# A chain of transformer-like stages on one core: order of the work at the norm boundaries, and which engine adds LayerNorm's mean

## The chip, the cores and the metric

One core of one Trainium2 chip. The metric is the time in microseconds (us) from start to end of one execution. The kernel holds a whole model of 21 stages in one program; its weights come from HBM piece by piece, while the activations (1024 features of 512 tokens) stay in SBUF.

## What is computed

Two stacks of two layers in fp32: the first with RMS norms in front of its mixers and FFNs, the second with LayerNorm behind each sum.

```python
def rms_norm(x, g):
    xf = x.astype(F32)
    y = xf * lax.rsqrt(jnp.mean(xf * xf, axis=-1, keepdims=True) + NORM_EPS)
    return (y * g.astype(F32)).astype(x.dtype)

def layer_norm(x, g, b):
    xf = x.astype(jnp.float32)
    mu = jnp.mean(xf, axis=-1, keepdims=True)
    var = jnp.mean(jnp.square(xf - mu), axis=-1, keepdims=True)
    return ((xf - mu) * lax.rsqrt(var + LN_EPS) * g + b).astype(x.dtype)

def swiglu_2(x, w_in, w_out):
    gu = x @ w_in
    g, u = gu[..., :D_FF], gu[..., D_FF:]
    return (jax.nn.silu(g) * u) @ w_out
...
    for l in range(DEPTH):
        x = layer_norm(ALPHA * x + 0.5 * swiglu_2(x, ffn_w_in[l, 0], ffn_w_out[l, 0]), ln_g[l, 0], ln_b[l, 0])
        j = l // N_MIXERS
        if l % N_MIXERS == 0:
            y = mlstm_mixer(x, ml_w_in[j], ml_gate_b[j], ml_norm_g[j], ml_w_out[j])
        else:
            y = window_attention(x, at_w_in[j], at_sink[j], at_w_out[j])
        x = layer_norm(ALPHA * x + y, ln_g[l, 1], ln_b[l, 1])
        x = layer_norm(ALPHA * x + 0.5 * swiglu_2(x, ffn_w_in[l, 1], ffn_w_out[l, 1]), ln_g[l, 2], ln_b[l, 2])
```

## The kernel before

Layout. Features lie on the 128 partitions, in KD = 8 tiles of 128; the T = 512 tokens lie on the free axis and are taken at a norm in two halves of 256 (HALVES). R holds the residual. Each fp32 operand is split into a high and a low part (XH and XL, HH and HL, WH and WL), and each product is three matmuls: lines 310, 311 and 312 (pe_three).

Weights come in units of 128 x 1024. SyncE loads unit n into a ring of RING = 6 places RAW once unit n - 6 is done (unit_done), ScalarE copies it to WH (hi_to, line 292), VectorE subtracts and writes WL over RAW (lo_to, line 298). Both keep count: hi_to(n) and lo_to(n) split what is missing up to unit n.

Stages: load, ev_attn, ev_mamba, n_ffn0, ffn0, n_mix1, od, n_ffn1, ffn1, n_final, f00, ln00, mlstm, ln01, f01, ln02, f10, ln10, win, ln11, f11. Nine are norms between other stages: n_ffn0, n_mix1, n_ffn1 and n_final are RMS norms, five are LayerNorms. Behind ("prod") ln00, ln02, ln10, n_mix1 and n_final stands an FFN, behind the others a mixer.

End of an FFN (ffn_pe, lines 465 to 482). down(m) multiplies the hidden features (22 k-tiles) into output tile m in three units, k-tiles 0 to 8, 8 to 16 and 16 to 22. The last tile (m = 7) is done once for each token half; between the first and the second unit of its second half TensorE does stats_pe (line 402): column sums of S1 and R (LayerNorm alone) and of S2 and the last SQ, against a matrix of ones, into PSUM banks 4 and 5. S1 and S2 are sums over the tiles that VectorE keeps in finish (line 688), SQ the squares that ScalarE makes (square_act, line 484). A mixer's output projection (outproj_pe) does its last three tiles by halves; stats_pe of half 0 stands behind the first of the second half.

The norm itself, per half h: VectorE waits for the sums, makes the variance (chain, line 830), ScalarE the reciprocal root (root, line 618), VectorE a Newton step and NB = -mean times root. Then for each tile t (0 to 7 in half 0, 8 to 15 in half 1), in a buffer XT of four places:
- VectorE: XT = R * RS (normed, line 854)
- LayerNorm alone, GpSimd: XT = XT + NB (line 549)
- ScalarE: R = g * XT + b where the residual is kept (line 633), XH = g * XT + b (line 635)
- VectorE: XL = R - XH (low, line 860; 862 in an RMS norm without keep)
- TensorE waits for x_ready of the tile

VectorE's order is written out in norm (line 847): three tiles of normed ahead, then normed(t + 3), low(t); behind t = 2 the last tile or tiles of the second half of the stage before (ffn_tail(1) or mixer_tail(1)); lo_to(nx + 4) behind t = 5; chain(e, 1) behind t = 7; lo_to(nx + 5) behind t = 10 and lo_to(nx + 6) behind t = 13. nx is the first unit of the next stage. ScalarE does hi_to at the same t, and the squares of the second half behind t = 3.

The next stage begins with first_units (line 334): three units together over half 0 (per k-tile 9 matmuls of 256 columns), stats_pe of half 1 behind k = 4, the fourth unit over half 0, then all four units over half 1 (12 matmuls per k-tile). Before each k-tile TensorE waits for its XL.

## Time and profile before

| what | us |
|---|---|
| median of 3 runs | 3537.15 (3535.1 to 3537.25) |
| time of the profiled execution | 3536.34 |
| its span, first to last instruction | 3534.5 |
| TensorE busy | 3431.3 (97%) |
| VectorE busy | 1842.6 (52%) |
| ScalarE busy | 1308.0 (37%) |
| GpSimd busy | 92.8 (3%) |
| mean granted TensorE clock | 0.991 |

Times in the rows further down are us from the start of the span. PE is TensorE, DVE is VectorE, ACT is ScalarE, POOL is GpSimd. A row of a timeline is start, duration, engine, line, operation, what it writes and reads, shape, count and, in brackets, the idle time before it and what ended it. Matmuls overlap, so that their pace is read from their starts.

### The profile page before, as it was taken

How to read it: one execution, taken by the hardware profiler on the slowest of the kernel's cores; microseconds unless marked ns; L12 is line 12 of the kernel's file. 1: busy time of each engine (PE TensorE's matmuls, PEld its weight loads, DVE VectorE, ACT ScalarE, POOL GpSimd, SP SyncE). 2: the span in 40 equal slices, each digit the busy share in tenths (PEclk: the TensorE clock that was granted, in tenths of full speed). 3: DMA queues.
4: the chain of work that ended last, by engine and by line, in shares of the span. 5: the costliest groups of instructions: out<-in, count | busy, mean ns of one | idle time of the engine just before them, and what ended most of it. 6: DMA issues, size and time to landing. Idle time of an engine off the chain costs nothing.

```text
span 3534.5 us, 43300 instructions
## 1 busy us (share of the span) xinstructions
PE 3431.3 (97%) x17564; PEld 2827.1 (80%) x17564; DVE 1842.6 (52%) x2925; ACT 1308.0 (37%) x2217; POOL 92.8 (3%) x133
## 2 busy tenths in 40 slices
PE   8999999999998999999999999999999999999998
PEld 7667778888876988898888768888888888788887
DVE  5775775433885644354435357443454336564446
ACT  4442443222465322242224344322242226543233
POOL 0000000000100000000001001000010001010000
PEclk9999999999999999999999999999999999999999
DMA  3102112323210222322332201232322331013245
GB/s 127 59 24 95 60 60 90 100 96 107 88 37 20 95 96 96 107 96 96 97 105 81 99 31 54 102 101 96 107 85 96 101 106 64 31 49 125 95 138 166
DMA packets 92506, 307.59 MB, mean 87 GB/s; under 512 B 16014, under 2 KB 17684, under 8 KB 92308
## 3 DMA queue, kind: packets, MB, share of 16 engines
q1 hardware_dynamic: 89528, 301.31, 25.4%
q10 hardware_dynamic: 2780, 3.51, 0.3%
q8 instruction: 140, 2.29, 0.3%
q14 instruction: 58, 0.48, 0.0%
HBM read 302.69 MB, written 2.10 MB: 86 GB/s over the span
## 4 chain that ended last, share of the span: by engine, by line
PE 82%; DVE 11%; ACT 4%; issue 2%; DMA 0%; SPq 0%; DVEq 0%; POOL 0%; ACTq 0%
PE ps L310 23%; PE ps L311 23%; PE ps L312 23%; PE ps L307 13%; DVE XT L854 1%; DVE WL L298 1%; ACT WH L292 1%; DVE mb_cv L1786 1%; PE ps L2768 1%; DVE XL L860 1%; DVE R L699 1%; DMA RAW<-units 0%; DVE S L708 0%; DVE mb_e L1847 0%; PE ps L1097 0%
## 5 line engine op out<-in xcount | busy, mean ns | idle before, releaser
L310 PE MATMUL ps<-XH,WH 128*128 128x512 f32 (+1 forms) x3200 | 1189.7, 372 | 34.2 <-DVE XL L860 23.6
L312 PE MATMUL ps<-XH,WL 128*128 128x512 f32 (+1 forms) x3200 | 1173.9, 367 | 0.0
L311 PE MATMUL ps<-XL,WH 128*128 128x512 f32 (+1 forms) x3200 | 1173.8, 367 | 0.0
L298 DVE TENSOR_TENSOR WL<-RAW,WH 128x1024 fp32r<-128x1024 f32 x567 | 688.3, 1228 | 313.8 <-ACT WH L292 310.1
L310 PEld LDWEIGHTS ps<-XH,WH 128*128 128x128 f32 x3200 | 609.0, 190 | 142.6 <-DVE XL L860 16.8
L312 PEld LDWEIGHTS ps<-XH,WL 128*128 128x128 f32 x3200 | 609.0, 190 | 97.3
L311 PEld LDWEIGHTS ps<-XL,WH 128*128 128x128 f32 x3200 | 609.5, 190 | 95.8 <-issue 1.9
L292 ACT ACTIVATE WH<-RAW 128x1024 fp32r<-128x1024 f32 x567 | 587.3, 1050 | 146.0 <-DMA RAW<-units 80.2
L310 PE MATMUL ps<-HH,WH 128*128 128x512 f32 (+1 forms) x990 | 362.8, 366 | 0.0
L311 PE MATMUL ps<-HL,WH 128*128 128x512 f32 (+1 forms) x990 | 361.9, 366 | 0.0
L312 PE MATMUL ps<-HH,WL 128*128 128x512 f32 (+1 forms) x990 | 361.9, 366 | 0.0
L589 ACT ACTIVATE HH<-HV 128x512 fp32r<-128x512 f32 x132 | 83.4, 632 | 566.2 <-DVE HV L773 566.2
L770 DVE SCALAR_TENSOR_TENSOR SG<-TH,ps 128x512 f32<-128x512 f32 x132 | 90.7, 687 | 299.4 <-ACT TH L586 299.2
L773 DVE SCALAR_TENSOR_TENSOR HV<-SG,ps 128x512 f32<-128x512 f32 x132 | 90.7, 687 | 297.0 <-PE ps L312 296.8
L699 DVE SCALAR_TENSOR_TENSOR R<-R,ps 128x512 f32<-128x512 f32 (+1 forms) x86 | 51.6, 599 | 361.2 <-PE ps L312 360.6
L490 ACT ACTIVATE SQ<-R 128x512 f32<-128x512 f32 (+1 forms) x89 | 49.0, 551 | 509.9 <-DVE R L699 432.1
L586 ACT ACTIVATE TH<-ps 128x512 f32<-128x512 f32 x132 | 78.7, 596 | 368.5 <-PE ps L312 368.5
L310 PEld LDWEIGHTS ps<-HH,WH 128*128 128x128 f32 x990 | 186.7, 189 | 30.3
L311 PEld LDWEIGHTS ps<-HL,WH 128*128 128x128 f32 x990 | 186.7, 189 | 30.3
L312 PEld LDWEIGHTS ps<-HH,WL 128*128 128x128 f32 x990 | 186.7, 189 | 30.0
L775 DVE TENSOR_TENSOR HL<-HV,HH 128x512 fp32r<-128x512 f32 x132 | 91.4, 693 | 101.4 <-ACT HH L589 101.4
L549 POOL TENSOR_TENSOR XT<-XT,NB 128x256 f32<-128x256 f32 x80 | 74.8, 949 | 2082.1 <-DVE XT L854 2082.1
(607 smaller groups left out, 3438.5 us busy)
## 6 DMA issues: line engine op xcount, KB each, us to landing
RAW<-units SPq DMA_DIRECT2D x567, 512.0 KB, 3.3
XIN<-in_x ACTq DMA_DIRECT2D x2, 1024.0 KB, 6.1
out<-YT SPq DMA_DIRECT2D x8, 256.0 KB, 3.1
GB<-in_ln_g SPq DMA_DIRECT2D x1, 512.0 KB
GB<-in_ln_b SPq DMA_DIRECT2D x1, 512.0 KB
da_pi<-in_positions ACTq DMA_DIRECT2D x1, 256.0 KB, 3.1
mb_pairf<-constants ACTq DMA_DIRECT2D x1, 256.0 KB
wa_dist<-constants ACTq DMA_DIRECT2D x1, 192.0 KB, 2.2
```

The lines of the kernel that those rows point to most:

```text
L292: nc.scalar.activation(WH[:, u % RING, :], RAW[:, u % RING, :], ACT.Copy).then_inc(S["wh_ready"], 1)
L298: nc.vector.tensor_tensor(WL[:, u % RING, :], RAW[:, u % RING, :], WH[:, u % RING, :].bitcast(F32), ALU.subtract)\
L307: return nc.tensor.matmul(out, lhsT, rhs, start=start, stop=stop, **kw)
L310: nc.tensor.matmul(out, wh, xh, start=start, stop=False)
L311: nc.tensor.matmul(out, wh, xl, start=False, stop=False)
L312: return nc.tensor.matmul(out, wl, xh, start=False, stop=stop)
L586: nc.scalar.activation(TH[:, j % 2, :], ps[:, 2 * (j % 3), :], ACT.Tanh, scale=0.5).then_inc(S["ffn_act"], 1)
L589: nc.scalar.activation(HH[:, j, :], HV[:, j % 2, :], ACT.Copy).then_inc(S["ffn_act"], 1)
L699: own(v.scalar_tensor_tensor(rk, rk, alpha, src, ALU.mult, ALU.add), "r_ready")
L770: own(v.scalar_tensor_tensor(SG[:, j % 2, :], TH[:, j % 2, :], 1.0, ps[:, b, :], ALU.add, ALU.mult))
L773: own(v.scalar_tensor_tensor(HV[:, j % 2, :], SG[:, j % 2, :], e["half"], ps[:, b + 1, :], ALU.mult, ALU.mult), "ffn_dve")
L775: own(v.tensor_tensor(HL[:, j, :], HV[:, j % 2, :], HH[:, j, :].bitcast(F32), ALU.subtract), "ffn_dve")
```

## The change

Four parts, all at the norm boundaries.
- down_parts: the last output tile of an FFN takes its short unit (k-tiles 16 to 22) first, in the list of units too. stats_pe of half 0 still stands behind the first unit.
- Sums and variance: stats_pe signals behind S1 and R and again behind S2 and SQ (stats_ready counts 4 per LayerNorm), and VectorE's first two operations wait for the first signal alone. square_added, the adding of tile 6's squares into S2, stands ahead of the wait for the last tile. stats_pe of half 1 stands behind k = 3 (FFN behind) or k = 5 (mixer behind) in a LayerNorm.
- NB is added by VectorE, and GpSimd's loop is gone. VectorE takes tiles in pairs (one operation over two tiles) but for the first two of each half; low is paired too in part.
- The order on VectorE and ScalarE is written out anew: hi_to(nx + 4) directly behind root(0), lo_to(nx + 4) after tile 4, 5 (LayerNorm) or after the variance of half 1 (RMS), lo_to(nx + 5) behind low(9).

```diff
@@ def down_parts
+def down_parts(m):
+    return ((16, 22), (0, 8), (8, 16)) if m == KD - 1 else ((0, 8), (8, 16), (16, 22))
@@ first_units
+            stats_at = 4 if not nrm.get("ln") else 3 if nrm["prod"]["kind"] == "ffn" else 5
...
-                elif k == 4:
+                elif k == stats_at:
                     stats_pe(pe, nrm, 1)
@@ stats_pe
-                mm(ps[:, 4, hs], ones[:], R[:, KD - 1, hs], False, True)
+                mm(ps[:, 4, hs], ones[:], R[:, KD - 1, hs], False, True).then_inc(S["stats_ready"], 1)
@@ ffn_pe
-                for q, (k0, k1) in enumerate(parts):
+                for q, (k0, k1) in enumerate(down_parts(m)):
@@ gpsimd
-                if e["kind"] == "norm" and e["ln"]:
-                    for t in range(16):
-                        x = XT[:, t % 4, :]
-                        pool.wait_ge(S["ln_scaled"], 16 * lns + t + 1)
-                        nc.gpsimd.tensor_tensor(x, x, NB[:, t // 8, :], ALU.add).then_inc(S["t_ready"], 1)
-                    lns += 1
@@ scalar, norm
                 root(0)
+                hi_to(act, nx + 4)
+                squares_at = 3 if not e["ln"] else 4 if prod["kind"] == "ffn" else 5
...
-                    if t == 3:
+                    if t == squares_at:
                         for q in range(KD, KD + prod["tail"]):
                             square_act(act, prod, q)
-                    if t in (5, 10, 13):
-                        hi_to(act, nx + {5: 4, 10: 5, 13: 6}[t])
+                    if t in (10, 13):
+                        hi_to(act, nx + {10: 5, 13: 6}[t])
@@ vector
                     else:
+                        square_added(e, KD - 2)
                         dve.wait_ge(S["tail_done"], e["t0"] + 1)
...
-            def chain(e, h):
+            def variance(e, h):
...
                 if e["ln"]:
+                    dve.wait_ge(S["stats_ready"], e["st0"] + 2 * h + 1)
                     own(v.tensor_scalar(a, s1, 1.0 / D, None, ALU.mult))
                     own(v.tensor_tensor(a, a, s1, ALU.mult))
+                    dve.wait_ge(S["stats_ready"], e["st0"] + 2 * h + 2)
                     own(v.scalar_tensor_tensor(x, s2, D * LN_EPS, a, ALU.add, ALU.subtract), "var_ready")
...
+                def normed(t, n=1):
                     k, h = t % 8, t // 8
+                    x = XT[:, t % 4:t % 4 + n, :]
+                    wide = lambda a: a[:, h:h + 1, :].to_broadcast([P, n, HT])
+                    own(v.scalar_tensor_tensor(x, R[:, k:k + n, HALVES[h]], D ** 0.5, wide(RS), ALU.mult, ALU.mult),
+                        None if ln else "t_ready")
+                    if ln:
+                        own(v.tensor_tensor(x, x, wide(NB), ALU.add), "t_ready", by=n)
...
+                variance(e, 0)
+                rooted(e, 0)
+                if ln:
+                    normed(0)
+                    normed(1)
+                    low(0)
+                    normed(2, 2)
+                    low(1)
+                    normed(4, 2)
+                    low(2)
+                    low(3)
+                    if ffn_behind:
+                        ffn_tail(1)(e["prod"])
+                        normed(6, 2)
+                        low(4, 2)
+                    else:
+                        mixer_tail(1, (0,))(e["prod"])
+                        low(4, 2)
+                        mixer_tail(1, (1, 2))(e["prod"])
+                        normed(6, 2)
+                    lo_to(dve, nx + 4)
+                    variance(e, 1)
+                    low(6, 2)
+                    rooted(e, 1)
+                    normed(8)
+                    normed(9)
+                    low(8)
+                    normed(10, 2)
+                    low(9)
+                    lo_to(dve, nx + 5)
+                    normed(12, 2)
+                    low(10, 2)
+                    normed(14, 2)
+                    low(12, 2)
+                    lo_to(dve, nx + 6)
+                    low(14, 2)
+                else:
+                    normed(0)
+                    for t in range(8):
+                        if t < 7:
+                            normed(t + 1)
+                        low(t)
+                        if t == 2:
+                            (ffn_tail if ffn_behind else mixer_tail)(1)(e["prod"])
+                    variance(e, 1)
+                    lo_to(dve, nx + 4)
+                    rooted(e, 1)
...
```

rooted(e, h) is the rest of chain: it waits for the root, does the Newton step and NB.

## Rows read from the trace of the kernel before

**Rows 1.** The page, busy time, share of the span, instructions of TensorE.
```profile
PE 3431.3 (97%) x17564; PEld 2827.1 (80%) x17564; DVE 1842.6 (52%) x2925; ACT 1308.0 (37%) x2217; POOL 92.8 (3%) x133
```

**Rows 2.** Waits of TensorE: for whom; us in total, times, longest.
```profile
PE ps L310 <- DVE XL L860: 23.6, 17, 2.4
...
PE ps L310 <- DVE XL L862: 3.0, 2, 2.7
```

**Rows 3.** Timeline of TensorE at ln00 (last rows ln01, ln02): start, us, instruction, idle before.
```profile
1902.41 0.28 PE L312 MATMUL ps<-HH,WL 128*128 128x256 f32 x1
1902.54 0.59 PE L307 MATMUL ps<-S,ones 128*128 128x256 f32 x2
...
1911.84 0.35 PE L310 MATMUL ps<-XH,WH 128*128 128x256 f32 x1 [2.39 <-DVE XL L860]
...
1928.08 0.39 PE L310 MATMUL ps<-XH,WH 128*128 128x256 f32 x1 [1.31 <-DVE XL L860]
...
1933.23 0.39 PE L310 MATMUL ps<-XH,WH 128*128 128x256 f32 x1 [0.57 <-DVE XL L860]
...
2212.74 0.39 PE L310 MATMUL ps<-XH,WH 128*128 128x256 f32 x1 [0.57 <-DVE XL L860]
...
2562.47 0.36 PE L310 MATMUL ps<-XH,WH 128*128 128x256 f32 x1 [2.38 <-DVE XL L860]
```

**Rows 4.** Timeline of VectorE at ln00, then ln01 and ln02.
```profile
1892.66 0.69 DVE L703 TENSOR_TENSOR S<-S,R 128x512 f32<-128x512 f32 x1
...
1901.78 1.22 DVE L298 TENSOR_TENSOR WL<-RAW,WH 128x1024 fp32r<-128x1024 f32 x1 [0.78 <-ACT WH L292]
1904.46 0.42 DVE L836 TENSOR_SCALAR VA<-ps 128x256 f32<-128x256 f32 x1 [1.45 <-PE ps L307]
...
1908.19 2.62 DVE L854 SCALAR_TENSOR_TENSOR XT<-R,RS 128x256 f32<-128x256 f32 x4
1911.26 0.42 DVE L860 TENSOR_TENSOR XL<-R,XH 128x256 fp32r<-128x256 f32 x1 [0.45 <-DVE XT L854]
...
1930.27 0.42 DVE L860 TENSOR_TENSOR XL<-R,XH 128x256 fp32r<-128x256 f32 x1
1930.73 1.64 DVE L298 TENSOR_TENSOR WL<-RAW,WH 128x1024 fp32r<-128x1024 f32 x1
...
1932.75 0.43 DVE L860 TENSOR_TENSOR XL<-R,XH 128x256 fp32r<-128x256 f32 x1
...
2177.86 2.36 DVE L298 TENSOR_TENSOR WL<-RAW,WH 128x1024 fp32r<-128x1024 f32 x2
...
2555.11 0.42 DVE L836 TENSOR_SCALAR VA<-ps 128x256 f32<-128x256 f32 x1 [1.46 <-PE ps L307]
...
2583.30 0.42 DVE L860 TENSOR_TENSOR XL<-R,XH 128x256 fp32r<-128x256 f32 x1
```

**Rows 5.** Timeline of ScalarE at ln00: root, XH, weight copy.
```profile
1905.83 0.42 ACT L621 ACTIVATE RS<-VA 128x256 f32<-128x256 f32 x1 [2.64 <-DVE VA L838]
...
1910.21 0.58 ACT L635 ACTIVATE XH<-XT,VEC 128x256 fp32r<-128x256 f32 x1
...
1929.00 1.05 ACT L292 ACTIVATE WH<-RAW 128x1024 fp32r<-128x1024 f32 x1
```

**Rows 6.** Timeline of GpSimd at ln00.
```profile
1908.77 3.51 POOL L549 TENSOR_TENSOR XT<-XT,NB 128x256 f32<-128x256 f32 x4 [888.58 <-DVE XT L854]
```

**Rows 7.** Windows: busy us of five engines, PEclk, DMA share, GB/s.
```profile
1890.00:1940.00 50.00, 45.74 (x345) 44.42 (x344) 37.10 (x61) 26.86 (x47) 14.91 (x16) 0.97 0.16 50
2170.00:2222.00 52.00, 46.62 (x331) 44.28 (x330) 42.95 (x73) 29.80 (x53) 14.96 (x16) 0.93 0.13 42
2548.00:2592.00 44.00, 39.29 (x299) 37.38 (x298) 33.16 (x56) 24.92 (x44) 14.96 (x16) 1.00 0.13 41
...
1120.80:1124.10 3.30, 3.30 (x9) 2.58 (x8) 0.00 (x0) 0.00 (x0) 0.00 (x0) 0.50 0.00 0
```

**Rows 8.** Timeline of TensorE in the stage od.
```profile
1119.27 0.50 PE L310 MATMUL ps<-od_gh,WH 128*128 128x512 f32 x1 [3.56 <-ACT od_y L2380]
```

**Rows 9.** The page, DMA issues: KB each, us from issue to landing.
```profile
RAW<-units SPq DMA_DIRECT2D x567, 512.0 KB, 3.3
```

More of the change, by code:

```diff
@@ L37, in knows, with __call__ @@
         self.n.update(dict.fromkeys(sems, 0))
-    def __call__(self, ins, name=None, wait=True):
+    def __call__(self, ins, name=None, wait=True, by=1):
         name = name or self.steps
-        ins.then_inc(self.sems[name], 1)
-        self.n[name] = self.n[name] + 1
+        ins.then_inc(self.sems[name], by)
+        self.n[name] = self.n[name] + by
         if wait:
@@ L72, in unit_lists @@
             for m in range(0 if s.get("last") else KD):
-                units += [tile(d, di, P * m, 0, 8), tile(d, di, P * m, 8, 16), tile(d, di, P * m, 16, 22)]
+                units += [tile(d, di, P * m, k0, k1) for k0, k1 in down_parts(m)]
         elif kind == "ev_attn":
@@ L703, in finish, with square_added @@
                     own(v.tensor_tensor(S1[:, hs], R[:, 0, hs] if m == 1 else S1[:, hs], rk, ALU.add))
-                if q and 0 < e["tiles"][q - 1][0] < KD - 1:
-                    m, h = e["tiles"][q - 1]
+                if not squares_in:
+                    square_added(e, q - 1)
+            def square_added(e, q):
+                if q >= 0 and 0 < e["tiles"][q][0] < KD - 1:
+                    m, h = e["tiles"][q]
                     hs = slice(0, T) if h is None else HALVES[h]
-                    dve.wait_ge(S["sq_ready"], e["sq0"] + q)
+                    dve.wait_ge(S["sq_ready"], e["sq0"] + q + 1)
                     own(v.tensor_tensor(S2[:, hs], SQ[:, 0, hs] if m == 1 else S2[:, hs], SQ[:, m % 2, hs], ALU.add), "s2_added")
@@ L714, in go, with mixer_tail @@
                     else:
+                        square_added(e, KD - 2)
                         dve.wait_ge(S["tail_done"], e["t0"] + 1)
-                    finish(e, KD - 1 + h, ps[:, 7 - h, HALVES[h]], e["alpha"])
+                    finish(e, KD - 1 + h, ps[:, 7 - h, HALVES[h]], e["alpha"], squares_in=True)
                 return go
-            def mixer_tail(h):
+            def mixer_tail(h, some=range(3)):
                 def go(e):
-                    for i in range(3):
+                    for i in some:
                         m = KD - 3 + i
@@ L843, in chain, with low @@
                 if e["ln"]:
-                    own(v.scalar_tensor_tensor(NB[:, h, :], s1, -(D ** -0.5), y, ALU.mult, ALU.mult))
+                    own(v.scalar_tensor_tensor(NB[:, h, :], ps[:, 4, HALVES[h]], -(D ** -0.5), y, ALU.mult, ALU.mult))
             def norm(e):
-                ln, final, nx = e["ln"], e["final"], e["next"]
-                def normed(t):
+                ln, nx = e["ln"], e["next"]
+                ffn_behind = e["prod"]["kind"] == "ffn"
+                def normed(t, n=1):
                     k, h = t % 8, t // 8
-                    if final and t >= 4:
-                        dve.wait_ge(S["norm_r"], e["nr0"] + t - 3)
-                    x = XT[:, t % 4, :]
-                    own(v.scalar_tensor_tensor(x, R[:, k, HALVES[h]], D ** 0.5, RS[:, h, :], ALU.mult, ALU.mult), "ln_scaled" if ln else "t_ready")
-                def low(t):
+                    x = XT[:, t % 4:t % 4 + n, :]
[4 more added lines that the diff above has]
+                        own(v.tensor_tensor(x, x, wide(NB), ALU.add), "t_ready", by=n)
+                def low(t, n=1):
                     k, hs = t % 8, HALVES[t // 8]
-                    dve.wait_ge(S["xh_ready"], 16 * e["c"] + t + 1)
+                    dve.wait_ge(S["xh_ready"], 16 * e["c"] + t + n)
                     if ln or e["keep"]:
-                        own(v.tensor_tensor(XL[:, k, hs], R[:, k, hs], XH[:, k, hs].bitcast(F32), ALU.subtract), "x_ready")
+                        own(v.tensor_tensor(XL[:, k:k + n, hs], R[:, k:k + n, hs], XH[:, k:k + n, hs].bitcast(F32), ALU.subtract),
+                            "x_ready", by=n)
                     else:
@@ L863, in low @@
                                                    XH[:, k, hs].bitcast(F32), ALU.mult, ALU.subtract), "x_ready")
-                ahead = 3 if ln and not final else 1
-                chain(e, 0)
-                for t in range(ahead):
-                    normed(t)
-                for t in range(16):
-                    if t + ahead < (8 if t < 8 else 16):
-                        normed(t + ahead)
-                    if not final:
-                        low(t)
-                    if t == 2:
-                        second.get(e["prod"]["kind"], mixer_tail(1))(e["prod"])
-                    if t == 5:
-                        lo_to(dve, nx + 4)
-                    if t == 7:
-                        chain(e, 1)
-                        for i in range(8, 8 + ahead):
-                            normed(i)
-                    if t in (10, 13):
-                        lo_to(dve, nx + {10: 5, 13: 6}[t])
+                variance(e, 0)
@@ new lines, in norm @@
+                rooted(e, 0)
[38 more added lines that the diff above has]
+                            normed(t + 1)
+                        low(t)
+                        if t == 2:
[3 more added lines that the diff above has]
+                    rooted(e, 1)
+                    normed(8)
+                    for t in range(8, 16):
+                        if t < 15:
+                            normed(t + 1)
+                        low(t)
+                        if t in (10, 13):
+                            lo_to(dve, nx + {10: 5, 13: 6}[t])
```

16 lines of the change are left out of this document (9 added, 7 removed).

## The prediction

> **What bounds the kernel now.** I read the page first, for the engine that fills the span: TensorE is busy 3431.3 of 3534.5 us [rows 1]. So only the some 100 us in which it waits can be won. The waits of TensorE come next: its longest entry is one helper line, L860, the low part XL of the normalised tiles, 23.6 us in 17 waits [rows 2]. L860 runs in the LayerNorms and in n_final; the RMS line L862 is worth 3.0 us in 2 waits. So the change works on some 24 us at five LayerNorm boundaries. Three have an FFN behind them (ln00, ln02, ln10), two a mixer (ln01, ln11).
>
> Then the time order of ln00. TensorE issues the column sums at 1902.54, works through its cover (14 k-tiles, 42 matmuls 0.12 us apart) and waits 2.39 us until XL of tile 0 is there; then 1.31 us before token half 1 and 0.57 us at its tile 3 [rows 3]. VectorE in the same time is a chain without room: variance, root, Newton, four scalings that take 2.62 us together, XL [rows 4]. ScalarE is the station between [rows 5]. GpSimd's first four adds last 3.51 us [rows 6]. A scaling takes 0.42 us alone and up to 0.84 us beside a GpSimd add (four take 2.62, not 4 x 0.46 = 1.84).
>
> What ends the boundary is the last of these waits. XL of tile 11 (half 1, k = 3) ends at 1932.75 + 0.43 = 1933.18, TensorE goes on at 1933.23 and has five tiles of 12 matmuls (1.43 us each) left: 1940.4. In a mixer boundary it is the same wait, at 2212.74 [rows 3].
>
> The clock: the windows of the boundaries read 0.97 for ln00, 0.93 for ln01 and 1.00 for ln02, the level lies at 0.50 in the stretch after a wait of 3.56 us elsewhere [rows 7, 8], and each low stretch costs some 1.7 us of matmul work (0.07 x 52 = 3.6 us for ln01's two). Yet this does not set the end today: from the variance to XL of tile 11 ln00 takes 1932.75 - 1904.46 = 28.29 us with a low stretch, ln02 2583.30 - 2555.11 = 28.19 us without one [rows 4]. VectorE sets the end, and a slow TensorE uses up its own waiting.
>
> **The change part by part, for ln00** (times of the trace; an operation of VectorE 256 wide counts 0.46 with its handing over, one 512 wide 0.72, from L703's 0.69 [rows 4]; XT to XH over ScalarE 0.03 + 0.50 + 0.58, and 0.10 back to VectorE [rows 5]).
>
> Short unit first: 18 matmuls stand ahead of the sums instead of 24, so they start 0.72 us sooner, at 1901.8. The cover grows by the same six matmuls and ends where it did, at 1909.3.
>
> Sums and variance sooner: the first two operations no longer wait for the squares, which would bring 0.9 us, but VectorE has a weight split until 1903.0 [rows 4]. So they run from 1903.0, the third from 1904.0. The variance is ready at 1904.4 instead of 1905.8: 1.4 us.
>
> Mean by VectorE: NB is ready at 1906.75. Scaling and add of tile 0 (2 x 0.46) end at 1907.6; GpSimd's ended near 1909.7, when ScalarE took over. XH is ready at 1908.7 and XL of tile 0 at 1909.25 (1911.68 before). TensorE's first wait of 2.39 us is gone.
>
> What is late next: now each pair of tiles costs VectorE 2 x 0.72 before the next XL. XL of tiles 1 and 2 come 1.91 us apart (1.45 + 0.46), and TensorE needs 1.08 us for a tile (9 matmuls): 0.83 us of waiting, twice. The squares and sums of half 1 move ahead (ScalarE squares after tile 4, TensorE sums after k = 3, near 1915.3), and VectorE takes the half's last tile before its pair 6, 7: hidden, since TensorE is busy with k = 1 to 3. XL of tiles 6 and 7 stands behind the variance of half 1: 0.4 us. Half 0 ends at about 1924.5, 2.2 us sooner than before, and half 1 starts without its 1.31 us.
>
> Half 1, k = 2: here I see a new wait. The order on VectorE is: normed(10, 2), low(9), lo_to(nx + 5), normed(12, 2), low(10, 2). The split in lo_to waits for its WH, which ScalarE makes after XH of tile 10. Behind that waiting split stand two wide operations and XL of 10 and 11, for which TensorE waits. In numbers: normed(10, 2) ends at 1925.3, XH of 10 at 1926.4, WH (1.04 us, [rows 5]) at 1927.4; the split (1.14) at 1928.6, the pair (1.45) at 1930.0, XL of 10 and 11 at 1930.74. TensorE wants tile 10 two tiles after 1924.5, at 1927.4: 3.4 us of waiting. Before, XL of tile 10 came at 1930.27 + 0.42 = 1930.69, ahead of the split: the same time. From 1930.8 six tiles are left, 8.6 us: 1939.4 against 1940.4. So 1.0 us is won at each FFN boundary, while the clock stays up.
>
> Mixer boundaries: the short unit does not exist there, and in ln01 VectorE has two splits until 2180.2, until after the sums are done [rows 4], so the variance is no sooner. The same steps from there give a first wait of 1.06 us, 0.83 twice, some 3 us before tiles 6 and 7 (they stand behind a variance whose sums TensorE issues only after its tile 5), XL of 10 and 11 at 2211.0 and the end at 2219.7 against 2212.74 + 5 x 1.43 = 2219.9: 0.2 us won.
>
> The clock after the new wait: a wait of 3.4 us is longer than all of these boundaries had. After the comparable one of 3.56 us the clock was 0.50 [rows 7, 8]. A low stretch costs about 1.7 us of work; now it lies behind the last wait, where nothing takes it up. I take 1.6 us for each of the five, bounds 0 (ln02 had a wait of 2.38 us [rows 3] and kept 1.00) and 3.3 (two stretches).
>
> ScalarE's early weight split (hi_to right behind root 0) waits for a DMA: issue to landing is 3.3 us [rows 9], issued when the short unit is done near 1902.0, so it lands near 1905.3 and the copy ends near 1906.3, before the first XT at 1907.6: cost 0, covered by the Newton steps. Should the DMA be 1.3 us later it would delay XH directly. SP's order and all DMA sizes stay. RMS boundaries: their order hardly moves, they wait 3.0 us together, the larger part behind a mixer's tail that stays where it is: 0, bounds -0.5 and +0.5 for all four.
>
> The pairs' price is not in the trace (512 elements in two rows of 256, one operand repeated). Bounds: two single operations, 0.84 + 0.07 us (nothing saved), and L703's 0.69. I take 0.69, the nearest row in size. The chain up to XL of tile 10 has 13 wide operations (five pairs scaled and shifted, three pairs of XL); at the upper bound each lasts 0.19 us more, up to 2.5 us per boundary, +12 us in all.
>
> The sum: 3 x 1.0 + 2 x 0.2 = 3.4 us won, 5 x 1.6 = 8.0 us lost to the clock: +4.6 us on the profiled execution's 3536.34, 3540.9. The median of the runs shown lies 0.8 us higher, so I say 3541.5 us, 0.12% slower than 3537.15. A measurement of this kernel can tell about 0.2%, 7 us, from no change.
>
> **The rivals.**
> (A) The new wait does not arise: XL of 10 and 11 gets there in time, because ScalarE is far enough ahead with WH. Then TensorE runs through from 1924.5: 8 x 1.43 gives 1936.0, 4.4 us won per FFN boundary and 3.6 per mixer boundary, 20.4 us: 3536.3 + 0.8 - 20.4 = 3517. For it: half 0 does run 2 us sooner, and VectorE loses all contention. Against: WH stands behind XH of tile 10 in ScalarE's order, and that needs normed(10, 2).
> (B) The clock costs nothing, as in ln02. Then 3.4 us stay won: 3533.5. Speaking for it is that 2.38 us of waiting there left the level at 1.00; against it the stretch behind 3.56 us. The Trainium skill (TensorE: Matmul & The Clock Gate, "What's actually happening") calls the low level the state of an idle array, which activity releases; read strictly, a wait between working stretches would cost no clock. By that rule it is this rival; ln00 and ln01, 0.97 and 0.93 with waits of at most 2.4 us, speak against the strict reading.
> (C) Slower: the clock falls twice per boundary. The two waits of 0.83 us in 2.8 us, and in the mixers a wait of 3 us, lie early in half 0. A low stretch there delays the sums of half 1 by up to 1.7 us; VectorE has about 1 us of room before its variance, and from there on the whole chain moves. It decides once more than that 1 us is lost. Price: 0.7 to 1.7 us more at each boundary, 3.5 to 8.5 in all: 3545 to 3550. The pairs at their upper bound would end in the same place.
> (D) The change does nothing that can be seen: the gain and the clock cancel, within 2 us of 3537. This lies within my own case.
>
> **How the numbers follow.** My case with (D): 0.45 (3535 to 3544.2); B: 0.12; A: 0.16; C: 0.27. B falls wholly within 0.2%, and A nearly wholly outside it. C begins at its very edge: 0.03 of it stay below 3544.2, and I give my own case 0.03 above (a second low stretch at some boundaries). Faster by over 0.2% (below 3530.1): A's 0.16 and 0.01 of B, 0.17. Slower (above 3544.2): 0.24 + 0.03 = 0.27. Within: the rest, 0.56. The range leaves out A and the far end of C: 3530 to 3549.
>
> **What would show it.** Right, if in the profile after: GpSimd is idle at the boundaries and scalings take 0.42 us; sums of ln00 start 0.7 us sooner; the first wait of an FFN boundary is near 0 and two of 0.8 us follow; VectorE idles 1.7 us before the split in half 1 and TensorE 3 us or more at tile 10; the clock of ln02's window falls from 1.00. Wrong, if TensorE shows no wait over 1 us in half 1 (then A), or if paired operations last over 0.8 us (then C), or if the windows keep 1.00 behind the long wait (then B). A sum that misses by more than 10 us with these waits all in place would mean that something outside the norms moved.

## The result and the profile after

| | before | after |
|---|---|---|
| median, us | 3536.24 (3533.1 to 3539.75, 22 runs) | 3542.55 (3539.57 to 3545.52, 22 runs) |
| profiled execution: time, span, us | 3536.34, 3534.5 | 3542.36, 3540.2 |
| GpSimd busy, us | 92.8 | 18.4 |
| TensorE's waits for XL of the normalised tiles (LN), us, times | 23.6, 17 | 31.1, 22 |

The changed kernel takes 1.0019 of the time of before, 95% interval 1.0013 to 1.0025: 6.3 us, or 0.18%, slower. The interval does not hold 1, but the difference is small for a kernel of this length. The forecast was 3541.5 us in a range of 3530 to 3549. GpSimd's adds are gone and so is the first long wait, and yet the time is longer. First the page, engine times, and the waits of TensorE (for whom; us in total, times, longest):

```profile
span 3540.2 us, 43231 instructions
...
PE 3430.6 (97%) x17564; PEld 2826.7 (80%) x17564; DVE 1833.7 (52%) x2920; ACT 1310.5 (37%) x2217; POOL 18.4 (1%) x53
```

```profile
PE ps L317 <- DVE XL L875: 31.1, 22, 3.4
```

L875 is L860 of before. Its longest wait was 2.4 us [rows 2] and is 3.4 now. Where the waits stand, at ln00 (and the last three rows at ln01), in the timeline of TensorE (start, us, instruction, idle before):

```profile
1900.28 0.38 PE L314 MATMUL ps<-S,ones 128*128 128x256 f32 x1
...
1910.11 0.39 PE L317 MATMUL ps<-XH,WH 128*128 128x256 f32 x1 [0.93 <-DVE XL L875]
...
1912.10 0.39 PE L317 MATMUL ps<-XH,WH 128*128 128x256 f32 x1 [0.65 <-DVE XL L875]
...
1930.14 0.39 PE L317 MATMUL ps<-XH,WH 128*128 128x256 f32 x1 [3.35 <-DVE XL L875]
...
1940.35 0.40 PE L317 MATMUL ps<-XH,WH 128*128 128x512 f32 x1
...
2201.46 0.39 PE L317 MATMUL ps<-XH,WH 128*128 128x256 f32 x1 [2.77 <-DVE XL L875]
...
2212.99 0.39 PE L317 MATMUL ps<-XH,WH 128*128 128x256 f32 x1 [3.35 <-DVE XL L875]
...
2223.21 0.40 PE L317 MATMUL ps<-XH,WH 128*128 128x512 f32 x1
```

The first wait of 2.39 us [rows 3] is gone, short ones follow, and half 1, which had waits of 1.31 and 0.57 us, has one of 3.35 us at its tile k = 2. Its cause is read from VectorE and ScalarE at the same place:

```profile
1924.53 0.42 DVE L875 TENSOR_TENSOR XL<-R,XH 128x256 fp32r<-128x256 f32 x1
1926.68 1.23 DVE L305 TENSOR_TENSOR WL<-RAW,WH 128x1024 fp32r<-128x1024 f32 x1 [1.72 <-ACT WH L299]
1927.82 0.69 DVE L866 SCALAR_TENSOR_TENSOR XT<-R,RS 128x512 f32<-128x512 f32 x1
1928.61 0.69 DVE L869 TENSOR_TENSOR XT<-XT,NB 128x512 f32<-128x512 f32 x1
1929.39 0.69 DVE L875 TENSOR_TENSOR XL<-R,XH 128x512 fp32r<-128x512 f32 x1
```

```profile
1925.04 0.59 ACT L636 ACTIVATE XH<-XT,VEC 128x256 fp32r<-128x256 f32 x1
1925.53 1.04 ACT L299 ACTIVATE WH<-RAW 128x1024 fp32r<-128x1024 f32 x1
```

The first of these two is XH of tile 10. ScalarE makes the weight's high part WH only behind it, VectorE's split (L305) waits 1.72 us for WH, and behind the waiting split stand the pair 12, 13 and the paired XL of 10 and 11, for which TensorE waits. XL of tile 10 could have been made as soon as its XH was there.

The windows of the three boundaries (busy us of PE, PEld, DVE, ACT, POOL with counts, PEclk, DMA share, GB/s), and the stretch behind the long wait of ln00:

```profile
1890.00:1940.00 50.00, 44.84 (x340) 43.44 (x339) 35.56 (x60) 27.50 (x47) 0.00 (x0) 0.97 0.15 46
...
2170.00:2222.00 52.00, 43.52 (x324) 41.48 (x323) 40.84 (x71) 29.35 (x51) 0.00 (x0) 0.97 0.10 35
...
2548.00:2592.00 44.00, 39.17 (x294) 37.81 (x294) 33.25 (x55) 26.73 (x46) 0.00 (x0) 0.96 0.12 41
...
1931.10:1934.40 3.30, 3.30 (x18) 3.30 (x17) 2.42 (x3) 3.23 (x6) 0.00 (x0) 0.50 0.22 45
```

Each of the five LayerNorm boundaries has one stretch of 3.4 us at the level 0.50 (1.2 of 2.4 GHz), which in this execution begins 0.8 to 1.3 us after TensorE goes on at tile 10. ln02, which read 1.00 before [rows 7], reads 0.96.

The measure from here on is the length of a boundary: from TensorE's first sum to its first matmul over all tokens behind the boundary, which is 512 columns wide (384 at ln10). Where the short unit comes first, the sums start 0.72 us sooner at an FFN boundary, and the lengths there are given with those 0.72 us taken off.

| us | ln00 | ln01 | ln02 | ln10 | ln11 |
|---|---|---|---|---|---|
| before | 37.99 | 42.08 | 37.89 | 45.08 | 41.85 |
| after | 39.35 | 43.79 | 39.00 | 46.10 | 43.56 |
| difference | +1.36 | +1.71 | +1.11 | +1.02 | +1.71 |

That is 6.9 us. The RMS boundaries give n_mix1 0.0, n_final -0.6, n_ffn1 +0.6 and n_ffn0 +1.4. The rest of the program makes up -2.6 us to the 5.7 us between the spans. Which of these belong to the change is said further down, with the prediction.

### The profile page after: what moved, and what is told of

Its sections match the earlier page's. It is cut to its first block, busy times and chain, and to the rows that moved or that the text cites. A ratio compares the mean times of both kernels' runs of the same rounds, so it can differ in the third digit from the quotient of the medians.

```text
span 3540.2 us, 43231 instructions
## 1 busy us (share of the span) xinstructions
PE 3430.6 (97%) x17564; PEld 2826.7 (80%) x17564; DVE 1833.7 (52%) x2920; ACT 1310.5 (37%) x2217; POOL 18.4 (1%) x53
## 3 DMA queue, kind: packets, MB, share of 16 engines
q8 instruction: 140, 2.29, 0.3%
## 4 chain that ended last, share of the span: by engine, by line
PE 83%; DVE 10%; ACT 5%; issue 2%; DMA 0%; SPq 0%; DVEq 0%; ACTq 0%
PE ps L317 23%; PE ps L318 23%; PE ps L319 23%; PE ps L314 13%; DVE WL L305 2%; ACT WH L299 1%; DVE mb_cv L1837 1%; DVE XT L866 1%; DVE XT L869 1%; PE ps L2819 1%; DVE R L700 1%; DVE XL L875 1%; ACT XH L636 0%; ACT R L634 0%; DVE S L713 0%
## 5 line engine op out<-in xcount | busy, mean ns | idle before, releaser
L317 PE MATMUL ps<-XH,WH 128*128 128x512 f32 (+1 forms) x3200 | 1189.2, 372 | 41.9 <-DVE XL L875 31.1
L305 DVE TENSOR_TENSOR WL<-RAW,WH 128x1024 fp32r<-128x1024 f32 x567 | 686.5, 1224 | 328.4 <-ACT WH L299 324.6
L636 ACT ACTIVATE XH<-XT,VEC 128x256 fp32r<-128x256 f32 x144 | 78.8, 550 | 28.5 <-DVE XT L866 28.4
```

The source lines that it names most:

```text
L305: nc.vector.tensor_tensor(WL[:, u % RING, :], RAW[:, u % RING, :], WH[:, u % RING, :].bitcast(F32), ALU.subtract)\
L317: nc.tensor.matmul(out, wh, xh, start=start, stop=False)
L636: nc.scalar.activation(XH[:, k, hs], XT[:, t % 4, :], ACT.Identity, scale=g, bias=b).then_inc(S["xh_ready"], 1)
```

## The experiments

Ratios are to the kernel before in runs on the same chip, whose median there was 3534.8 us (split behind, filler, short unit, mean alone), 3535.79 us (the next four) and 3534.74 us (filler in before). The changed kernel's own 1.0019 comes from the 22 runs above. A boundary is stated as its difference to the kernel that was edited.

**The split behind XL of 10 and 11.** The changed kernel with the split in half 1 moved behind, and its copy on ScalarE one tile sooner:

```
-                    if t in (10, 13):
-                        hi_to(act, nx + {10: 5, 13: 6}[t])
+                    early = 9 if e["ln"] else 10
+                    if t in (early, 13):
+                        hi_to(act, nx + {early: 5, 13: 6}[t])
...
                     low(9)
-                    lo_to(dve, nx + 5)
                     normed(12, 2)
                     low(10, 2)
+                    lo_to(dve, nx + 5)
```

> The changed kernel, with one thing moved at the LayerNorms: VectorE's weight split of unit nx + 4 stands behind XL of tiles 10 and 11 instead of ahead of them, and ScalarE makes its WH behind tile 9 instead of behind tile 10. Theory (the queued split makes the wait at tile 10 and the low clock stretch behind it): the five waits of 3.35 us fall to about 0.9, and some 0.5 us of waiting at tile 12 comes new; 2.1 us per boundary from the waits and 1.7 us from the clock, 19 us in all: 3524 us, ratio to the kernel before 0.9965. Rival B (a low clock stretch costs nothing): 10.5 us, 3532, ratio 0.999. Rival (the added time lies in half 0 or outside the LayerNorms): no change from 3542.5, ratio 1.002.

(The split that is moved is that of unit nx + 5, as the edit says.)

Measured: 3526.24 us (3525.54 to 3527.63), ratio 0.9976, interval 0.9967 to 0.9985. All five boundaries are 3.57 us (ln00 to ln10) or 3.58 us (ln11) shorter than after, 17.9 us in all where 19 was expected. The interval leaves out both the expected 0.9965 and rival B's 0.999. TensorE, then VectorE, at ln00:

```profile
1930.08 0.39 PE L317 MATMUL ps<-XH,WH 128*128 128x256 f32 x1 [0.70 <-DVE XL L876]
...
1933.53 0.39 PE L317 MATMUL ps<-XH,WH 128*128 128x256 f32 x1 [0.30 <-DVE XL L876]
```

```profile
1929.34 0.69 DVE L876 TENSOR_TENSOR XL<-R,XH 128x512 fp32r<-128x512 f32 x1 [0.27 <-ACT XH L636]
1930.06 1.23 DVE L305 TENSOR_TENSOR WL<-RAW,WH 128x1024 fp32r<-128x1024 f32 x1
```

The window of ln00 reads 1.00 again:

```profile
1892.50:1942.50 50.00, 47.19 (x357) 45.02 (x356) 35.56 (x60) 29.47 (x50) 0.00 (x0) 1.00 0.20 68
```

So two instructions in the wrong order carried the whole loss and more. With them swapped the same change is a gain of 8.6 us over before. At the FFN boundaries the 3.57 us are the wait that shrank from 3.35 to 0.70 + 0.30 us (2.35 us); the other 1.2 us go with the low stretch that no longer comes. In the mixers the wait at tile 10 is gone whole, and a low stretch now lies at the wait of 2.76 us at tile 6. The edit moves two things at once. An estimate for VectorE's move alone, from the rows after: XH of tile 11 ends at 1927.55, so XL of 10 and 11 would end near 1928.3 instead of 1930.1, 1.7 us sooner; the rest needs ScalarE's copy out of the way too.

**Matmuls in the wait.** To price the clock by itself, TensorE is given 27 matmuls without use (27 x 0.12 = 3.2 us) in the wait at tile 10 of the changed kernel:

```
             for k in range(KD):
+                if k == 2 and nrm.get("ln"):
+                    for q in range(27):
+                        mm(ps[:, 7, HALVES[0]], w_of(n0, 0)[0], XH[:, 0, HALVES[0]])
```

> The changed kernel, with 27 matmuls of 256 columns more at each LayerNorm, issued by TensorE just ahead of its wait for tile 10 into a bank that nobody reads, 0.12 us each: they fill 3.2 of the 3.35 us in which it waits. Nothing else moves. This is the price of the clock by itself. Theory (each of the five low stretches behind that wait costs 1.7 us): the windows behind tile 10 read 1.00 and the time falls by 8.5 us: 3534 us, ratio to the kernel before 0.9995. Rival B (the clock costs nothing): same as the changed kernel, 3542.5, ratio 1.002. If the filler delays TensorE, it is longer.

Measured: 3537.02 us, ratio 1.0005 (0.9996 to 1.0014), against 1.0019 for the change. The boundaries are 1.48 us shorter four times and 0.54 once (ln11, where a low stretch came in half 0), 6.5 us in all where 8.5 was expected. TensorE at ln00 no longer waits, and the windows of ln00 and ln02 read 1.00:

```profile
1932.93 0.40 PE L314 MATMUL ps<-XH,WH 128*128 128x256 f32 x2
1933.44 0.39 PE L317 MATMUL ps<-XH,WH 128*128 128x256 f32 x1
```

```profile
1893.30:1943.30 50.00, 48.09 (x374) 46.51 (x373) 35.57 (x60) 28.59 (x49) 0.00 (x0) 1.00 0.17 52
...
2546.70:2590.70 44.00, 42.42 (x333) 41.05 (x332) 33.24 (x55) 26.69 (x46) 0.00 (x0) 1.00 0.12 40
```

VectorE's chain is unchanged here, and XL of tile 10 comes no sooner. What went away is the price of one low stretch: 1.48 us here, 1.2 us by the subtraction of the last experiment. This rules out rival B, in which the clock was free.

Another run shows the same price without any filler. The kernel with the late RMS copy (further on) has the code of the changed kernel in all LayerNorms, but in its execution the low stretch of ln01 began at 2202.3, at the wait of 2.77 us at tile 6. TensorE then came later to tile 10, waited 1.94 us there instead of 3.35, and no low stretch followed:

```profile
2202.30:2205.60 3.30, 3.10 (x14) 3.10 (x15) 3.06 (x8) 0.36 (x1) 0.00 (x0) 0.50 0.00 0
```

```profile
2214.02 0.38 PE L317 MATMUL ps<-XH,WH 128*128 128x256 f32 x1 [1.94 <-DVE XL L878]
```

ln01 lasts 42.29 us there and ln11 42.08, 1.5 us less than in the table above, while ln00, ln02 and ln10 agree with it to 0.1 us. So at a mixer boundary the same code paid for its low stretch in one execution and not in another.

**The same matmuls in the kernel before.** If every low stretch cost this much, those of before would have been worth removing too. The claim in the prediction was that they are free there. 18 matmuls (13 in a mixer) go ahead of the first wait:

```
+            if nrm.get("ln"):
+                for q in range(18 if nrm["prod"]["kind"] == "ffn" else 13):
+                    mm(ps[:, 0, HALVES[0]], w_of(n0, 0)[0], WH[:, n0 % RING, 0:HT])
```

> The kernel before with filler matmuls of 256 columns, 0.12 us each, issued by TensorE just ahead of its wait for tile 0 at the LayerNorms: 18 behind an FFN (2.15 of 2.38 us), 13 behind a mixer (1.55 of 1.8 us). Nobody reads their result. Theory (before the change VectorE's chain sets the end of these boundaries, and a low clock stretch in half 0 runs into waits that stand there anyway): the low stretches at tile 0 go, the boundaries end when they did behind an FFN and at most 1 us sooner behind a mixer, where the sums of half 1 are nearer to the edge; 0 to 2 us in all, ratio 1.000. Rival (each low stretch costs its 1.5 us wherever it lies): 6 to 9 us less, ratio 0.998.

Measured: 3536.12 us, ratio 1.0003 (0.9994 to 1.0012). ln00 is -0.06 us, ln02 +0.05, ln10 +0.08, ln01 -0.50 and ln11 -0.33, although ln00 and ln10 lost their one low stretch, and ln01 and ln11 one of their two (ln02 had none). The window of ln00 reads 1.00 instead of 0.97:

```profile
1890.00:1940.00 50.00, 47.51 (x365) 45.44 (x364) 37.12 (x61) 27.50 (x48) 14.93 (x16) 1.00 0.14 46
```

```profile
1927.44 0.39 PE L310 MATMUL ps<-XH,WH 128*128 128x256 f32 x1 [1.71 <-DVE XL L863]
```

TensorE is done with half 0 sooner and waits 1.71 us before half 1 where it waited 1.31 [rows 3]. The gain of the clock turned into waiting, as the prediction said, at ln00 and ln10 to within 0.1 us.

**The short unit first, alone.** The kernel before with `down_parts` and nothing else:

```
+    return ((16, 22), (0, 8), (8, 16)) if m == KD - 1 else ((0, 8), (8, 16), (16, 22))
```

> The kernel before with the short unit first alone (down_parts, in the list of units and in the down projection); the order on VectorE, the signals and GpSimd's adds stay. Theory (at a LayerNorm behind an FFN VectorE's chain from the sums to XL of tile 11 sets the end, so what the sums win arrives whole): 0.7 us at each of three boundaries, 2.1 us less than the kernel before, ratio 0.9994; in RMS norms nothing. Rival (covered): 0, ratio 1.000.

Measured: 3534.77 us, ratio 0.9999 (0.999 to 1.0008); the interval holds both the 2.1 us expected and nothing. The boundaries say more: -0.54, -0.69 and -0.69 us at ln00, ln02 and ln10, -0.48 at ln11 and +0.90 at ln01. The two rows show ln00's first wait, 1.66 us where it was 2.39 [rows 3], and the second wait of ln01, 2.78 us where it was 1.53:

```profile
1909.35 0.35 PE L315 MATMUL ps<-XH,WH 128*128 128x256 f32 x1 [1.66 <-DVE XL L863]
...
2195.02 0.58 PE L315 MATMUL ps<-XH,WH 128*128 128x256 f32 x1 [2.78 <-DVE XL L863]
```

The 0.7 us come where they were expected. n_final, for which nothing was expected, is 0.60 us shorter as well. At ln01, which the edit does not touch, a low stretch of 6.8 us lies at that wait (the matmul lasts 0.58 us), the sums of half 1 come 0.87 us later, and the boundary is 0.90 us longer. (ln11, untouched as well, is 0.48 us shorter.)

**The mean on VectorE, alone.** The kernel before, each tile scaled and added singly by VectorE:

```
-                    own(v.scalar_tensor_tensor(x, R[:, k, HALVES[h]], D ** 0.5, RS[:, h, :], ALU.mult, ALU.mult), "ln_scaled" if ln else "t_ready")
+                    own(v.scalar_tensor_tensor(x, R[:, k, HALVES[h]], D ** 0.5, RS[:, h, :], ALU.mult, ALU.mult), None if ln else "t_ready")
+                    if ln:
+                        own(v.tensor_tensor(x, x, NB[:, h, :], ALU.add), "t_ready")
```

> The kernel before with one part alone: VectorE adds NB, each tile by itself, directly behind its scaling; GpSimd's loop is gone; order, units and signals stay as before. Theory: VectorE no longer loses time beside GpSimd (scalings 0.42 us), but has 16 operations of 0.46 us more per LayerNorm, and three tiles are scaled and shifted ahead of the first XL: XL of tile 0 comes 0.6 us later than before, XL of tile 11 1.4 us later behind an FFN and 0.2 us sooner behind a mixer: +4 us, ratio 1.001, up to +8 with clock stretches that the longer waits bring. Rival (contention is the dearer): faster by 0.4 us per tile that ran beside GpSimd, some 10 us, ratio 0.997.

Measured: 3549.1 us, ratio 1.0041 (1.0028 to 1.0053), 14.3 us slower than before: a miss. The boundaries are +1.44, +2.91, +1.54, +2.51 and +2.42 us. By form (line, operation, count, busy us, mean ns, idle us), first the scaling of the kernel before, then scaling and add of this one:

```profile
L854 DVE SCALAR_TENSOR_TENSOR XT<-R,RS 128x256 f32<-128x256 f32 x144 | 81.8, 568 | 4.4
```

```profile
L847 DVE SCALAR_TENSOR_TENSOR XT<-R,RS 128x256 f32<-128x256 f32 x144 | 61.1, 425 | 4.4
...
L849 DVE TENSOR_TENSOR XT<-XT,NB 128x256 f32<-128x256 f32 x80 | 34.0, 426 | 2.7
```

A scaling is cheaper once GpSimd is silent: 425 against 568 ns, 20.7 us in all. (The 568 are a mean over all 144; the 80 of the LayerNorms alone took 684.) The XL beside GpSimd gain too, 6.7 us. For this 34.0 us of adds come in, on the engine that sets the end. ln00 and ln02 are longer by what was expected, 1.4 us. The miss is in the mixers, +2.9 and +2.4 us where -0.2 was expected, and at ln10, and there the sums of half 1 come 1.6 to 2.0 us later (0.7 and 1.2 at ln00 and ln02), behind low stretches of 3.4 or 6.8 us. How much of it the clock costs was not separated. The boundaries give 10.8 of the 14.3 us; the rest was not looked into. At ln01:

```profile
2173.70:2225.70 52.00, 44.23 (x315) 42.51 (x314) 42.25 (x87) 28.61 (x50) 0.00 (x0) 0.90 0.10 31
...
2201.00:2204.30 3.30, 3.30 (x14) 3.07 (x14) 1.86 (x3) 1.49 (x4) 0.00 (x0) 0.50 0.00 0
```

```profile
2199.05 0.58 PE L310 MATMUL ps<-XH,WH 128*128 128x256 f32 x1 [3.24 <-DVE XL L855]
```

```profile
2205.67 0.42 DVE L829 TENSOR_SCALAR VA<-ps 128x256 f32<-128x256 f32 x1 [2.65 <-PE ps L307]
```

The window reads 0.90. A low stretch of 6.8 us begins in half 0, within a wait of 3.24 us, and VectorE then waits 2.65 us for the sums of half 1: the mechanism of rival C, in a kernel in which nothing else was moved.

**The mean back to GpSimd in the changed kernel.** The opposite edit: the new order, pairs scaled by VectorE, the mean added singly by GpSimd.

```
                     own(v.scalar_tensor_tensor(x, R[:, k:k + n, HALVES[h]], D ** 0.5, wide(RS), ALU.mult, ALU.mult),
-                        None if ln else "t_ready")
-                    if ln:
-                        own(v.tensor_tensor(x, x, wide(NB), ALU.add), "t_ready", by=n)
+                        "ln_scaled" if ln else "t_ready", by=n)
```

> The changed kernel with one part undone: GpSimd adds NB again, tile by tile; order, pairs of scalings, signals and short unit stay. Theory (in this order the XL stand directly behind the pairs, so VectorE waits for GpSimd, while the wait at tile 10 is made by the queued split and stays): XL of tile 0 0.5 us later, tile 10 some 1 us later, +5 us over the changed kernel: 3547, ratio to the kernel before 1.003. Rival (VectorE's adds are what cost the time, contention is cheaper): ratio below 1.000.

Measured: 3557.41 us, ratio 1.0065 (1.0052 to 1.0077), against 1.0019 for the changed kernel: some 16 us more, where 5 was expected. The boundaries are longer by 3.0, 2.2, 2.2, 3.2 and 2.8 us. Scaling and add by form:

```profile
L873 DVE SCALAR_TENSOR_TENSOR XT<-R,RS 128x512 f32<-128x512 f32 x30 | 24.2, 806 | 2.6
...
L555 POOL TENSOR_TENSOR XT<-XT,NB 128x256 f32<-128x256 f32 x80 | 71.2, 912 | 2106.3 <-DVE XT L873 2106.3
```

```profile
1929.24 1.23 DVE L305 TENSOR_TENSOR WL<-RAW,WH 128x1024 fp32r<-128x1024 f32 x1 [2.78 <-ACT WH L299]
```

A pair of adds takes GpSimd 2 x 0.91 us where VectorE takes 0.69, so XH of tile 10 is later and the split's wait grows from 1.72 to 2.78 us; TensorE's wait at tile 10 is 4.04 us. So in this order GpSimd is the wrong engine, and in the order of before VectorE is (previous experiment). Neither is better as such.

**Pairs taken apart.** The changed kernel, `normed(t, 2)` and `low(t, 2)` made of two single steps each.

> The changed kernel with its order, but every pair of VectorE taken apart into two operations 256 wide (scalings, adds and XL). Theory (a pair is worth what the fixed part of two operations costs, about 0.15 to 0.2 us each): the waits at tiles 1 and 2 grow from 0.6-0.9 to 1.2 us, the wait at tile 10 stays near 3 us; 0.9 us longer behind an FFN, 0.5 us behind a mixer, +3.6 us over the changed kernel's 3542.5: 3546, ratio to the kernel before 1.003. Rival (pairs are no gain, since a wide scaling is followed by 0.10 us instead of 0.03): 1.002 as the changed kernel.

Measured: 3543.67 us, ratio 1.0025 (1.0015 to 1.0035). The interval holds the changed kernel's 1.0019 as well as the expected 1.003. The boundaries are longer by 0.25, 0.28, 0.61, 0.57 and 0.06 us, 1.8 us in all, half of what was expected. TensorE's waits for XL (us in total, times, longest):

```profile
PE ps L317 <- DVE XL L883: 30.3, 27, 2.5
```

Pairing saves VectorE time, but it also makes TensorE wait for the second tile when it needs the first. The wait at tile 10 is even shorter with single steps, 2.51 us. So pairing was worth 0.1 to 0.6 us a boundary, and the low clock came behind 2.5 us as well as behind 3.4.

**The early weight copy at RMS boundaries.** The changed kernel, the copy of `hi_to(nx + 4)` at RMS norms back behind t = 5:

```
-                hi_to(act, nx + 4)
+                if e["ln"]:
+                    hi_to(act, nx + 4)
...
+                    if t == 5 and not e["ln"]:
+                        hi_to(act, nx + 4)
```

> The changed kernel with ScalarE's first weight copy put back behind tile 5 in the RMS norms alone. Theory (the copy directly behind the root waits for its DMA and holds up XH of tile 0): XL of tile 0 at n_ffn1 comes 5.0 us after the sums instead of 5.6, the wait at its tile 3 is 0.3 us again instead of 0.95, 0.6 us in all; nothing that the time can tell. Rival: 0.95 us stays, it is the mixer's tail.

Measured in one run: n_ffn1 lasts 31.07 us against 31.71 after, XL of tile 0 comes 4.99 us behind the sums against 5.62, and TensorE waits 0.32 us against 0.95. The next kernel, which has the same edit, gives 31.07 us too. (One time, 3540.25 us, says nothing about 0.6.) The row that shows why is ScalarE's of the changed kernel at n_ffn1:

```profile
1176.80 1.06 ACT L299 ACTIVATE WH<-RAW 128x1024 fp32r<-128x1024 f32 x1 [1.62 <-DMA RAW<-units]
1177.77 0.89 ACT L636 ACTIVATE XH<-XT,VEC 128x256 fp32r<-128x256 f32 x2
```

The copy waits for its DMA, and XH of tile 0 is queued behind it.

**Better orders.** If the order on VectorE is what decides, a better one must win. N is `normed`, L `low`, S a split, T a part of the tail, V and R variance and root of half 1, a number the tile (or split), p a pair:

```
+FFN_ORDER = "N0p N2p L0 T0 L1 S4 N4p L2p N6p L4p V L6p R N8 N9 L8 N10p L9 N12 L10 L11 N13 L12 N14p L13 S5 L14 L15 S6"
+MIX_ORDER = "N0p T0 N2p L0p S4 N4p L2p T1 T2 N6p L4p V L6p R N8 N9 N10 L8 L9 N11 L10 N12p L11 L12 N14p L13 L14 L15 S5 S6"
...
-            stats_at = 4 if not nrm.get("ln") else 3 if nrm["prod"]["kind"] == "ffn" else 5
+            stats_at = 4 if not nrm.get("ln") else 0 if nrm["prod"]["kind"] == "ffn" else 3
...
-                hi_to(act, nx + 4)
-                squares_at = 3 if not e["ln"] else 4 if prod["kind"] == "ffn" else 5
+                where = (5, 10, 13) if not e["ln"] else (-1, 3, 14) if prod["kind"] == "ffn" else (1, 10, 14)
+                squares_at = 3 if not e["ln"] else 2 if prod["kind"] == "ffn" else 4
```

> The changed kernel with a new order of VectorE and ScalarE at the LayerNorms, laid out by the durations of the traces: both first pairs are scaled ahead of the first XL, the squares and sums of half 1 move ahead (sums behind tile 0 or 3), the splits stand behind the XL that TensorE waits for, ScalarE's copies behind tile 3 or 10 and behind 14; in RMS norms ScalarE's first copy is back behind tile 5. Theory (the waits are a matter of order): an FFN boundary keeps some 1.4 us of waiting, a mixer boundary some 4.5 us, and none stands in half 1; 5.9 us less than the changed kernel at each, 29 us in all: 3513 us, ratio to the kernel before 0.993. Rival (VectorE's work is the bound whatever the order): no more than the first run with the split behind, 0.9976.

Measured: 3515.52 us (3513.0 to 3518.34), ratio 0.9944 (0.9931 to 0.9956), 20 us below before: the fastest of all. TensorE's waits for XL fall from 31.1 to 8.9 us:

```profile
PE ps L321 <- DVE XL L881: 8.9, 6, 3.0
```

```profile
1907.97 0.36 PE L321 MATMUL ps<-XH,WH 128*128 128x256 f32 x1 [0.88 <-DVE XL L881]
```

At an FFN boundary 0.88 + 0.11 us of waiting are left, at a mixer boundary some 3. Against the split-behind kernel the boundaries are 2.59, 2.29, 2.23 and 2.64 us shorter, but ln10 is 0.64 us longer, which the expectation did not have. TensorE behind ln10's last tile:

```profile
2948.36 0.51 PE L318 MATMUL ps<-WH,XH 128*128 128x256 f32 x1 [2.39 <-ACT wa_k L2868]
...
2949.09 0.41 PE L318 MATMUL ps<-WH,XH 128*128 128x256 f32 x1
```

The mixer there needs wa_k from ScalarE, which is ready only 0.9 us sooner, while TensorE comes 2.3 us sooner: its wait grew from 0.99 to 2.39 us, with a low stretch behind it, in which matmuls are 0.21 us apart instead of 0.12. Whether the wait of some 3 us left at each mixer boundary can be won was not tried.

## Why the prediction was right, and where its sizes were off

**What bounds, and what the change removes.** Right. Sums 0.72 us sooner, the variance 1.5 us sooner against the same work (1.4 said), XL of tile 0 7.44 us behind the sums where 1909.25 - 1901.8 = 7.45 was worked out, and the first wait gone. Then 0.93 (0.59 at ln02 and ln10) and 0.65 us where 0.83 twice was said, and 0.22 us at tile 6 where it was 0.4. In the mixers 0.87, 0.58, 0.65 and 2.77 us for 1.06, 0.83, 0.83 and 3.

**The new wait.** Right in place and cause: moving the two instructions removed it. Its size, 3.35 us for 3.4, is right because two errors cancel. At ln02 TensorE comes to tile 10 26.14 us behind the sums, where 1927.4 - 1901.8 = 25.6 was worked out, and XL comes 0.5 us late as well. Rival A needed that move. ScalarE's WH behind XH of tile 10 was the step that decided, and it is read from the diff and the order of two engines, not from the trace alone.

**What half 1 brings.** Mis-sized. XL of tiles 10 and 11 ends 29.46 us behind the sums at ln02, where 1930.74 - 1901.8 = 28.94 was worked out: 0.5 us. The term is the wide operation, taken at 0.69 + 0.03 us. It lasts 0.69, but where the next instruction reads its result it starts 0.10 us later:

```profile
2565.10 0.69 DVE L866 SCALAR_TENSOR_TENSOR XT<-R,RS 128x512 f32<-128x512 f32 x1
2565.89 0.69 DVE L869 TENSOR_TENSOR XT<-XT,NB 128x512 f32<-128x512 f32 x1
2566.62 0.88 DVE L875 TENSOR_TENSOR XL<-R,XH 128x256 fp32r<-128x256 f32 x2
```

From scaling to add 0.79 us, from add to the next operation 0.73: 0.07 us more in each of the five pairs, and as much where an XL follows its pair directly. So 0.4 to 0.5 us of the 1.0 us won at an FFN boundary were never there. It lies inside the bounds of the range (0.19 us each).

**The clock.** Right in kind, near in size. In the profiled execution one stretch per boundary, directly behind the wait, where nothing takes it up: 1.2 to 1.48 us measured for 1.6 taken. By the rule of the Trainium skill (TensorE: Matmul & The Clock Gate, "What's actually happening") that an idle array is at the low level and activity releases it, rival B had 0.12; the traces disagree with the strict reading, since in the changed kernel the low stretch begins 0.8 to 1.3 us after work is taken up again and ends while TensorE works. The prediction also took each stretch to lie behind the last wait. In the mixers that is chance: in the kernel with the late RMS copy it lay at tile 6 and cost nothing. That low stretches of before cost nothing at FFN boundaries was right as well; in the mixers, where one of two went, the boundaries became 0.3 and 0.5 us shorter, which the prediction had not separated.

**The sum at each boundary.** Said: +0.6 at an FFN boundary and +1.4 at a mixer boundary, 4.6 in all. Measured: +1.36, +1.11, +1.02 and twice +1.71, 6.9. The 0.5 us of the wide operations explain the FFN boundaries ln02 and ln10. ln00 has 0.25 us more, with the idle row below. A mixer boundary without its low stretch behind tile 10 is 0.2 us longer than before, where 0.2 us won was said.

**ScalarE's early copy, cost 0.** Right at the LayerNorms, where XL of tile 0 came when it was worked out, wrong at n_ffn1, by 0.6 us. The step took "RMS boundaries: their order hardly moves" for granted. There XT is ready earlier, without a mean to subtract, so the copy that waits 1.62 us for its DMA is in front of XH. The prediction had named the case ("Should the DMA be 1.3 us later it would delay XH directly") and not tried it against the RMS norms. It lies just beyond the bounds of 0.5 us for all four.

**n_final.** -0.6 us, a term taken at 0. The short unit alone gives -0.60 us there too, so it is the short unit's gain, which the prediction had put at 0 with the words "RMS boundaries: their order hardly moves".

**n_ffn0.** +1.4 us, with a low stretch of 6.8 us at 538.3 where before has one of 3.4 us at 540.4. This is not the change. Five kernels have the changed kernel's code at this boundary (itself, split behind, filler, pairs apart, mean on GpSimd): it lasts 36.34, 36.26, 35.03, 34.85 and 34.87 us, and the two long ones are the two with a low stretch of 6.8 us. The four with the code of before have 34.75 to 34.95 us. What makes the stretch longer in some executions stays open.

**Rival C.** It did not come in the changed kernel. But two experiments show its mechanism: the mean alone on VectorE (a wait of 3.24 us, then sums 2.65 us late) and the short unit alone (+0.90 us at ln01). The chance of 0.27 was for a real mechanism.

Forecast and result agree to about 1 us partly by luck. The forecast stood on the median of three runs of before, 3537.15 us, which 22 runs put at 3536.24; so +4.4 us was forecast against +6.3 measured. In the profiled executions the errors cancel: boundaries 2.3 us too low, n_ffn0 and n_ffn1 2.0 us not foreseen, n_final -0.6 and -2.6 us elsewhere on the other side. The -2.6 us lie in four stretches that the change does not touch, and kernels with the same code there differ as much:

| us | before | after | all kernels with the same code |
|---|---|---|---|
| start to the sums of n_ffn0 | 527.8 | 526.2 | 526.2 to 529.0 |
| od | 248.6 | 247.3 | 247.2 to 249.3 |
| mlstm | 237.4 | 239.1 | 237.4 to 240.9 |
| f11 | 352.1 | 350.7 | 350.7 to 352.1 |

So of the 5.7 us between the two spans, the LayerNorm boundaries behind an FFN (+3.5), n_ffn1 (+0.6) and n_final (-0.6) are the change's: the other kernels with the same code there repeat them to 0.2 us. The mixers' +3.4 hang on where the low stretch falls.

## What to carry to other kernels

An instruction that waits holds everything queued behind it. When an order is written out by hand, take each waiting instruction, note which other engine's queue its input stands in, and put what the bottleneck needs in front of it: here two lines moved turned a loss of 6 us into a gain of 9. Here a long wait on TensorE could be paid twice, with itself and with a low clock behind it (1.5 us), and the second part cost nothing where another wait stood further on to take it up. An engine's share of the work is cheap or dear only together with the order around it: the same add cost 14 us on VectorE in the order of before and some 16 us on GpSimd in the new one.
